# A row gate folded into the down projection's weights, in the two feed-forward blocks of a float32 program

## The reference

```
hin = x * (1 + sc2) + sh2
y = _swiglu(hin, ffn_w_in[i], ffn_w_out[i])          # (silu(gate) * up) @ w_out
x = _layernorm(DEEPNORM_ALPHA * x + (1 + gt2) * y, ln_g[i, 1], ln_b[i, 1])
```

## Time and profile before

| | |
|---|---|
| median of 3 runs | 3128.85 us (3121.71 to 3137.18) |
| the profiled execution | 3123.55 us |
| its span on the core | 3121.8 us |
| PE, DVE, ACT, POOL busy | 84%, 64%, 30%, 16% of the span |
| granted TensorE clock, mean | 0.926 of full speed |
| first feed-forward block | about 652 to 1084 us of the span |
| second feed-forward block | about 1482 to 1914 us |

### The profile page before, as it was taken

The page is one execution under the profiler, slowest core; times in us unless marked ns, Lnnn a source line. Parts: engine busy times, 40 slices in busy tenths (PEclk is TensorE's granted clock), DMA queues, the critical chain, the costliest instruction groups (busy, mean ns, idle before and its releaser), DMA issues. The chain is left out here.

```text
span 3121.8 us, 41213 instructions
## 1 busy us (share of the span) xinstructions
PE 2637.2 (84%) x16425; PEld 1923.8 (62%) x16425; DVE 1983.2 (64%) x2679; ACT 924.7 (30%) x999; POOL 488.7 (16%) x246
## 2 busy tenths in 40 slices
PE   5999888849999589776799993998894599999991
PEld 3444888337778444443577783896543488888870
DVE  7581666767663528433677536786623599999983
ACT  2101111112220021440222101343200477777761
POOL 0000000120000310002000003000000256656642
PEclk8998999979999899998899996999996699999995
DMA  4210121256652281000765433231306399999963
GB/s 177 80 71 33 57 71 71 109 177 185 184 161 101 103 265 54 1 1 28 223 186 174 134 104 130 81 95 54 135 14 254 113 359 364 369 362 356 357 246 124
DMA packets 248302, 481.05 MB, mean 154 GB/s; under 512 B 31734, under 2 KB 195086, under 8 KB 232809
## 3 DMA queue, kind: packets, MB, share of 16 engines
q1 hardware_dynamic: 227256, 453.59, 41.5%
q0 software_dynamic: 14368, 23.79, 2.2%
q10 hardware_dynamic: 6546, 1.79, 0.3%
HBM read 472.70 MB, written 36.85 MB: 163 GB/s over the span
## 5 line engine op out<-in xcount | busy, mean ns | idle before, releaser
L49 PE MATMUL ffn_bank<-ffn_xT_high,ffn_wi_high 128*128 128x512 f32 x704 | 281.1, 399 | 5.2 <-ACT ffn_xT L309 3.2
L51 PE MATMUL ffn_bank<-ffn_xT_high,ffn_wi_low 128*128 128x512 f32 x704 | 275.2, 391 | 0.0
L50 PE MATMUL ffn_bank<-ffn_xT_low,ffn_wi_high 128*128 128x512 f32 x704 | 275.2, 391 | 0.0
L303 ACT CAST ffn_wi_high<-ffn_wi 128x2048 fp32r<-128x2048 f32 x44 | 84.0, 1910 | 382.0 <-DMA ffn_wi<-in_ffn_w_in 302.0
L383 DVE SCALAR_TENSOR_TENSOR ffn_nsum<-ffn_nw,ffn_cond,ffn_nsum 128x256 f32<-128x256 f32 x336 | 162.9, 485 | 12.0
L49 PEld LDWEIGHTS ffn_bank<-ffn_xT_high,ffn_wi_high 128*128 128x128 f32 x704 | 132.8, 189 | 53.4 <-issue 16.6
L2735 POOL DMA_INDIRECT expert_rows<-exp_ys,exp_to_row x32 | 155.8, 4870 | 45.1 <-issue 44.3
L43 DVE TENSOR_TENSOR moe_g_low<-moe_g,exp_g_high 128x4096 fp32r<-128x4096 f32 x32 | 141.6, 4425 | 30.2 <-ACT exp_g_high L2810 30.2
L51 PEld LDWEIGHTS ffn_bank<-ffn_xT_high,ffn_wi_low 128*128 128x128 f32 x704 | 132.8, 189 | 28.6
L43 DVE TENSOR_TENSOR moe_u_low<-moe_u,exp_u_high 128x4096 fp32r<-128x4096 f32 x32 | 141.6, 4425 | 13.1 <-ACT exp_u_high L2810 13.1
L2810 ACT CAST exp_g_high<-moe_g 128x4096 fp32r<-128x4096 f32 x32 | 116.5, 3641 | 112.5 <-PE exp_p_g L51 83.2
(11 more groups left out here) (599 smaller groups left out, 6172.3 us busy)
## 6 DMA issues: line engine op xcount, KB each, us to landing
moe_g<-in_w_e_gate SPq DMA_DIRECT2D x32, 2048.0 KB, 10.0
moe_u<-in_w_e_up SPq DMA_DIRECT2D x32, 2048.0 KB, 9.8
moe_d<-in_w_e_down SPq DMA_DIRECT2D x32, 2048.0 KB, 9.7
ffn_wi<-in_ffn_w_in SPq DMA_DIRECT2D x88, 512.0 KB, 5.2
ffn_nw<-in_ada_w SPq DMA_DIRECT2D x24, 1024.0 KB
ffn_nw<-in_w_ada SPq DMA_DIRECT2D x24, 1024.0 KB
ffn_wo<-in_ffn_w_out SPq DMA_DIRECT2D x44, 512.0 KB, 3.3
hyb_wb<-in_w_in SPq DMA_DIRECT2D x20, 1024.0 KB, 5.8
```

The costliest lines, as they stand in the source:

```text
L49: nc.tensor.matmul(out, w[0], x[0], start=start, stop=False, **kw)
L50: nc.tensor.matmul(out, w[0], x[1], start=False, stop=False, **kw)
L51: return nc.tensor.matmul(out, w[1], x[0], start=False, stop=stop, **kw)
L303: nc.scalar.copy(wi_high[h][:, :, :, :], wi[h][:, :, :, :]).then_inc(s["wi_highs"], 1)
```

## The change

The gate is multiplied into the float32 weights in place before they are split, in `split_out`. One is added to `gt` in the head, after the second `split_in` and before the multiplication of `cond`. `deepnorm_rows` gets no `gt` in the two feed-forward blocks: the multiplication into `y` is gone there, and the scaled sum reads the PSUM bank directly.

```diff
@@ -357,6 +357,8 @@
                 def split_out(f):
                     slot = f % WO_RING
                     dve.wait_ge(wo_loaded[slot], f // WO_RING * 16 + 16)
+                    nc.vector.tensor_tensor(wo[slot][:, :], wo[slot][:, :], gt[:, :], ALU.mult).then_inc(s["wo_gated"], 1)
+                    dve.wait_ge(s["wo_gated"], f + 1)
                     nc.vector.tensor_copy(wo_high[slot][:, :], wo[slot][:, :]).then_inc(s["wo_highs"], 1)
@@ -392,6 +394,8 @@
                 split_in(1, 1)
+                dve.wait_ge(s["v_loaded"], 16 * 3)
+                link(nc.vector.tensor_scalar(gt[:, :], gt[:, :], 1.0, None, ALU.add))
                 dve.wait_ge(s["sig_done"], 1)
@@ -419,10 +423,8 @@
                 for f in range(2, NF):
                     split_out(f)
-                dve.wait_ge(s["v_loaded"], 16 * 3)
-                link(nc.vector.tensor_scalar(gt[:, :], gt[:, :], 1.0, None, ALU.add))
                 dve.wait_ge(s["x_again_loaded"], 16 * NT)
-                deepnorm_rows(nc, dve, link, lambda t, j: bank[2 * t + j], s["y_psum"], x_again, gt, y, st, mv, rstd,
+                deepnorm_rows(nc, dve, link, lambda t, j: bank[2 * t + j], s["y_psum"], x_again, None, y, st, mv, rstd,
                               s["var_done"], s["root"], s["scaled"])
@@ -432,8 +434,11 @@
             dve.wait_ge(y_psum, 2 * t + j + 1)
-            link(nc.vector.tensor_tensor(y[:, t, cols], bank_of(t, j)[:, :], gt[:, cols], ALU.mult))
-            link(nc.vector.scalar_tensor_tensor(out=y[:, t, cols], in0=x[:, t, cols], scalar=ALPHA, in1=y[:, t, cols],
+            branch = bank_of(t, j)[:, :]
+            if gt is not None:
+                link(nc.vector.tensor_tensor(y[:, t, cols], branch, gt[:, cols], ALU.mult))
+                branch = y[:, t, cols]
+            link(nc.vector.scalar_tensor_tensor(out=y[:, t, cols], in0=x[:, t, cols], scalar=ALPHA, in1=branch,
                                                 op0=ALU.mult, op1=ALU.add))
```

More of the change, by code:

```diff
@@ L141, in swiglu @@
         names = """x_loaded ident_loaded sc_loaded v_loaded sc_done xT_psum xT_done xT_split hidden sil_done act_done down_used
-                   y_psum steps root var_done scaled g_done normed stored wi_highs wi_split wo_highs wo_split act_steps
+                   y_psum steps root var_done scaled g_done normed stored wi_highs wi_split wo_gated wo_highs wo_split act_steps
                    x_again_loaded cond_loaded sig_done cond_done nsteps nsum_done n_psum nrow_done"""
```

## The result

Nine runs of the changed kernel have a median of 3109.1 us (3100.8 to 3112.7), nine of the kernel before, beside them, 3126.2 (3121.7 to 3137.2). The ratio is 0.9941, 95% interval 0.9927 to 0.9956: the kernel got faster, by 13.8 to 22.8 us. The changed kernel, run again unedited as a control in another set, came out at 0.9962 (0.9946 to 0.9979), 10.5 us by the medians. The profiled execution took 3103.29, of which the span is 3101.6; before it was 3121.8.

The account below looks back on a forecast made before the run. Barriers close the stages; PE bounds the down projection, DVE and POOL the rows after it. Two blocks gaining 7.59 less 0.73 at the head give 13.7 us, from the median 3128.85 to 3115.1 us; range 3105 to 3125.

Parts of the forecast that it names:

- rival 1: Rows, t = 1 to 3: L440 does not wait for POOL, L443 does; 18.3 us gain, 3110.6 us; chance 0.33.
- Two instructions at 0.73 go: First row tile, t = 0, without POOL work beside it: the removed multiplication saves 1.45 us.
- I expect it to run beside POOL as L435 does: Rows, t = 1 to 3: the scaled sum reading PSUM takes 0.69 us beside POOL, not 2.47.
- Rival 2: Rows: the sum from the bank still waits for POOL; only t = 0 gains, 1.5 us, 3127.4; chance 0.08.
- I take the wait, because L1321 is the nearest row: Rows, t = 1 to 3: L440 waits for POOL's instruction to end; a tile takes 6.15 us, not 8.22.
- L443 is the same operation, 64 times as wide, so it waits: Rows: L443, the same operation as L1321, waits for POOL if it meets POOL's work.
- So the 1.27 is hidden: Last down-projection split: PE's wait grows from 1.50 to 2.77 us, at no cost; otherwise 1.27 for a block.
- Rival 3: PE's clock falls to half for the 78 matmuls after the last split's wait; 13 us loss, 3142; chance 0.04.
- Under PE: Steady down projection: DVE's split grows from 1.9 to 3.2 us, still covered by PE's 5.41 for one f.
- 0.73 lost in each block: Head: the moved addition to gt delays the chain PE waits for, costing 0.73 us in each block.
- my bound of 1.7 for a longer low clock: Head: about 1.7 us more lost if PE's 0.50 clock after its idle time stays low for as long again.
- From x_again's landing to POOL's end: Sign in the rows: 28.0 us under the forecast, 25.7 if only L443 waits, 34.1 if the sum still waits.

Follow-up runs that it names:

- experiment 1: Changed kernel, but DVE first copies each PSUM bank into y, so the scaled sum reads both operands from SBUF again; 3130.6 us, ratio 1.0007.
- experiment 4: Changed kernel plus an extra SBUF scratch multiplication of 1 to 16 values per partition before the addition of epsilon in the rows; one run, 3109.6 us.
- experiment 2: Changed kernel without the added gate multiplication in the splits, so no gate at all in the feed-forward blocks; 3107.5 us, ratio 0.9941.
- Experiment 10: Changed kernel with the gate multiplication in the splits made twice; one run, 3122.0 us, blocks 430.0 and 429.7.
- experiment 3: Changed kernel with the addition of one to gt moved from the head to just before the split of tile 0; one run, 3105.8 us.
- experiment 6: Changed kernel with x_again loaded early, after w_out's tile 10, still with four slots; one run, 3106.3 us.

## Why the prediction was right or wrong

**Direction, mechanism and size.** The median of 3109.1 lies in the range, 6 below the forecast's 3115.1, which was counted from a median of 3128.85 where nine runs now give 3126.2. The forecast was a gain of 13.7 us; the two sets gave 17.1 and 10.5 by their medians, one beyond the 0.5% (15.6 us) that the prediction counts with and one short of it, and the blocks 17.9. The totals alone can't choose between 13.7 and rival 1's 18.3; the rows do, for rival 1. Of the 6 us, 2.7 are the other median of the kernel before. So the mechanism of the gain was right and one step of the working was not; that the time still lies in the range is no credit to that step, which is worth 4.6 us in a total that scatters by some 15.

**"Two instructions at 0.73 go", t = 0: right.** From the landing to L448's end it is 52.80 - 48.23 = 4.57, before 54.22 - 48.18 = 6.04: 1.47, against 1.45.

**"I expect it to run beside POOL as L435 does": right,** 0.69 in all sixteen; that it is the cause is shown by experiment 1, and agrees with the same line's SBUF calls in the changed kernel. Rival 2 falls. The rule in the Trainium skill, SBUF — State Buffer, "Who interferes with whom", by which a Vector instruction contends with GpSimd when both inputs are in SBUF, agrees: 0.69 with one of them in PSUM, 2.48 with both in SBUF.

**"I take the wait, because L1321 is the nearest row": wrong, and the one step of the rows' working that failed.** L445 is 0.15 beside POOL. L1321 handles 16 values for a partition, L440 one, and experiment 4 puts the border between one and two. That width was the only difference I had named, and I let the nearer operation decide. It cost the forecast (9.87 - 7.59) x 2 = 4.6 us. With it right, the working is rival 1's: 9.87 - 0.73 = 9.14 a block, measured 8.7 and 9.2.

**"L443 is the same operation, 64 times as wide, so it waits": right.** Its end comes 0.55 after POOL's, as rival 1 took over from L436. Its length of 1.8 shows only where PE is in time (experiment 2, the control's second block); in the profiled execution PE is late, and 0.81 to 1.09 is all that is seen.

**"So the 1.27 is hidden": nearly right, with less room than I gave it.** PE's wait grew to 2.85 and 2.79 (2.8 said). But PE ended at 1065.68, not 1063.77: 0.32 from its start, the rest from the low clock behind the wait. I had written that "one or two short stretches cost nothing there". In the profiled execution DVE did wait for PE three times, and the first block's rows take 26.29 where kernels with PE in time take 25.9: 0.4 us. Rival 3's start came, its length did not: the clock was low for about 4 us, not for the 78 matmuls. Experiment 10 shows the same wait, 0.9 and 1.3 longer, no more hidden.

**"Under PE" in the steady part: right,** and with 1.27 to spare for each f (experiment 10).

**The head: "0.73 lost in each block": 0.75 measured,** but it shows in PE's first wait at L237, 1.06 for 0.33, and not as "PE's wait at L237 4.5", which stays 3.77. In the first block the clock is also at 0.50 for longer: the stretch from 694.5 to 698.0 has 0.50 after and had 0.89 before. But that does not come with the addition. Here is that stretch in the kernel before, then its counterpart in experiment 3, where the addition is out of the head again:

```profile
694.50:698.00 3.50, 3.50 (x16) 2.78 (x15) 3.27 (x7) 0.00 (x0) 0.00 (x0) 0.89 0.94 307
```

```profile
694.00:697.50 3.50, 3.50 (x9) 2.69 (x9) 3.25 (x8) 0.00 (x0) 0.00 (x0) 0.50 0.94 304
```

It is 0.50 there too, with PE's second wait 3.76 as before; and in the first block of experiment 4, with the addition in the head, the clock is back at 0.88 from 694.06 to 696.06, 3 to 5 us behind the start of the second L237, where the changed kernel has 0.50. So my bound of 1.7 for a longer low clock can't be laid to the change. At the first sum the two blocks are 0.5 and 0.4 later than before, less than the start of the stage scatters. That a delay ahead of L237 is not made up agrees with the stretches under experiment 3.

**From x_again's landing to POOL's end:** 25.7 under rival 1; measured 26.29 and 25.98, and 25.88 to 25.92 in the three blocks in which DVE does not wait for PE (experiment 2 and the control's second).

Not tried: rows without POOL's part in t = 0 to 2, and a down projection that runs wholly at the low clock.

## What to carry to other kernels

Before moving an elementwise factor, look at which operands its consumer will then have: a sum with one operand in PSUM ran beside POOL, the same sum from SBUF waited for the end of every POOL instruction it met, and that was most of the gain; the two instructions saved show as 1.45 us in the first tile only. Work it out tile by tile until the next limit, and expect two limits at one pace: here POOL at 5.39 and PE at 5.44, so taking the lateness off PE moved the rows by 0.4 us at most (POOL's side was not tried), while loads issued earlier, the small addition put back behind the head and the last tile's tail on the idle engine gave another 16 us together in the blocks (22 by the medians). When the nearest row differs from the operation in a size, name the size as the open point and give both outcomes nearly equal weight.

## What the runs showed of the hardware that I had not expected

- A `tensor_scalar` from SBUF to SBUF with one value for each partition does not wait for POOL (0.15); with 2, 3, 4, 8 or 16 it ends 0.02 to 0.03 after POOL's instruction (2.03, 1.23, 1.91, 1.82, 1.83 long).
- The same idle time of PE, 2.80, was followed by a clock of 0.70 in one block and by 1.00 in the other of one execution. Over all the kernels with such a wait before tile 21, the clock fell behind nine of twelve waits of 2.39 to 2.89 and stayed at 1.00 behind three (2.80 in the control, 2.75 in experiment 4, 2.39 in experiment 6); it stayed behind all four of 1.50 to 1.65 and fell behind 3.79 and 4.09. What decides it between these no run here shows.
- POOL's addition is longer where it starts while DVE's sum is still at work: 2.75 in experiment 1, where it starts at 1054.10 and the sum ends at 1054.57, and 2.74 in the earlier trace rows, against 2.41 for the same one in the changed kernel. A DVE operation that only waits beside POOL does not lengthen it: 2.41 beside the waiting sum in experiment 1 (1051.61), beside L446 in experiment 2 and beside the probe of w = 2 in experiment 4. This is read from the rows; no run varied it alone.
